# Hybrid recurrent decoder step: columns and decays read in place, TensorE's filler groups moved, the mLSTM mask between two corner updates

## The reference

```python
# mLSTM: qc, kc, vc of a chunk, stabilised decays w, wi, ws
wqk = w * einsum('bthd,bshd->btsh', qc, kc)
num = einsum('btsh,bshd->bthd', wqk, vc) + wi * einsum('bthk,bhkv->bthv', qc, C)
den = sum(wqk) + wi * einsum('bthk,bhk->bth', qc, n)
h = num / max(abs(den), 1)
C = decay * C + einsum('bsh,bshk,bshv->bhkv', ws, kc, vc)
# gated delta rule
lmat = where(strict, einsum('bhtk,bhsk->bhts', kb, kh) * exp(diff), 0)
sol = triangular_solve(eye + lmat, [v * beta, kb * exp(g)])   # unit lower triangular
v_new = u - wk @ S
o = (q * exp(g)) @ S + attn @ v_new
S = S * exp(gl) + (k * exp(gl - g))^T @ v_new
# HGRN2
o = (q * exp(G)) @ S + attn @ v;   S = exp(Gl) * S + (k * exp(Gl - G))^T @ v
```

## Time and profile before

| what | value |
|---|---|
| runs, median (lowest to highest) | 3650.18 us (3647.09 to 3650.99) |
| profiled execution: its own time | 3649.81 us |
| profiled execution: its span | 3648.0 us |
| busy over the span, PE / DVE / ACT / POOL | 90% / 50% / 39% / 12% |
| `prompt_mixers`, tiles 0 to 15 in the trace | about 985 to 1740 us of the span |

### The profile page before, as it was taken

The page is one execution under the profiler, slowest core; times in us unless marked ns, Lnnn a source line. Parts: engine busy times, 40 slices in busy tenths (PEclk is TensorE's granted clock), DMA queues, the critical chain, the costliest instruction groups (busy, mean ns, idle before and its releaser), DMA issues. The chain is left out here.

```text
span 3648.0 us, 52370 instructions
## 1 busy us (share of the span) xinstructions
PE 3287.7 (90%) x21605; PEld 2988.0 (82%) x21605; DVE 1829.2 (50%) x2931; ACT 1416.9 (39%) x2100; POOL 436.4 (12%) x450
## 2 busy tenths in 40 slices
PE   5899999998289999897559979999999999999998
PEld 4899999998278888886538769999999999999987
DVE  6232333221378888885447734454454454454465
ACT  6233422322155555552025533343343343343454
POOL 0000000000156556651300000000000000000000
PEclk6899999999699999998579989999999999999999
DMA  5222233221622223221135564334444354344353
GB/s 194 50 60 67 70 72 83 83 71 57 255 76 93 96 89 98 88 75 44 39 138 214 186 234 163 133 144 153 149 173 153 118 186 150 133 146 154 133 202 116
DMA packets 232386, 450.24 MB, mean 123 GB/s; under 512 B 41383, under 2 KB 115293, under 8 KB 228029
## 3 DMA queue, kind: packets, MB, share of 16 engines
q1 hardware_dynamic: 230020, 428.33, 34.9%
q10 hardware_dynamic: 2128, 18.56, 1.4%
HBM read 363.38 MB, written 83.47 MB: 122 GB/s over the span
## 5 line engine op out<-in xcount | busy, mean ns | idle before, releaser
L2769 PE MATMUL ff_p<-ff_h_hi,ff_w_hi 128*128 128x384 f32 (+1 forms) x1536 | 502.6, 327 | 23.4 <-DMA ff_h_lo<-tmp_h 23.4
L2771 PE MATMUL ff_p<-ff_h_hi,ff_w_lo 128*128 128x384 f32 (+1 forms) x1536 | 502.8, 327 | 0.0
L2770 PE MATMUL ff_p<-ff_h_lo,ff_w_hi 128*128 128x384 f32 (+1 forms) x1536 | 501.9, 327 | 0.0
L412 PE MATMUL pin_pz<-hi,pin_whi 128*128 128x424 f32 (+1 forms) x1320 | 469.4, 356 | 14.2 <-DVE pin_wlo L528 14.2
L413 PE MATMUL pin_pz<-lo,pin_whi 128*128 128x424 f32 (+1 forms) x1320 | 467.2, 354 | 0.0
L414 PE MATMUL pin_pz<-hi,pin_wlo 128*128 128x424 f32 (+1 forms) x1320 | 467.0, 354 | 0.0
L2788 PE MATMUL ff_p<-ff_w_lo,ff_f_hi 128*128 128x512 f32 (+1 forms) x1088 | 426.7, 392 | 0.0
L2789 PE MATMUL ff_p<-ff_w_hi,ff_f_lo 128*128 128x512 f32 (+1 forms) x1088 | 426.4, 392 | 0.0
L2787 PE MATMUL ff_p<-ff_w_hi,ff_f_hi 128*128 128x512 f32 (+1 forms) x1088 | 423.8, 389 | 0.0
L2872 DVE TENSOR_TENSOR ff_w_lo<-ff_w,ff_w_hi 128x1024 fp32r<-128x1024 f32 x192 | 235.2, 1225 | 345.6 <-ACT ff_w_hi L2820 345.6
L2820 ACT ACTIVATE ff_w_hi<-ff_w 128x1024 fp32r<-128x1024 f32 x192 | 203.6, 1060 | 388.9 <-PE ff_p L2789 384.6
(11 more groups left out here) (522 smaller groups left out, 5536.5 us busy)
## 6 DMA issues: line engine op xcount, KB each, us to landing
ff_w<-in_w_unit SPq DMA_DIRECT2D x192, 512.0 KB, 5.2
ff_w<-in_w_unit SPq DMA_DIRECT2D x48, 2048.0 KB, 7.9
tmp_z<-pin_z SPq DMA_DIRECT2D x32, 1024.0 KB, 5.2
mix_rb<-tmp_rows_p SPq DMA_DIRECT2D x16, 1152.0 KB, 5.9
pin_w<-in_w_in SPq DMA_DIRECT2D x33, 512.0 KB, 8.1
gat_wa<-in_w_ada ACTq DMA_DIRECT2D x8, 2048.0 KB, 28.7
mix_zb<-tmp_z SPq DMA_DIRECT2D x16, 640.0 KB, 4.2
tmp_h<-op_h_hi SPq DMA_DIRECT2D x17, 512.0 KB, 4.1
```

The lines of the kernel that those rows point to most:

```text
L412: pe.matmul(pz[:, g, 0:n], whi[:, u, k], hi[:, k, at:at + n], start=(k == 0), stop=False)
L2769: pe.matmul(dst, w1_hi[:, u, k], hi, start=(k == 0), stop=False)
L2770: pe.matmul(dst, w1_hi[:, u, k], lo, start=False, stop=False)
L2771: mm = pe.matmul(dst, w1_lo[:, u, k], hi, start=False, stop=(k == KT - 1))
```

## The change

Four things change, all inside `prompt_mixers`. The arithmetic is the same.

1. `cc` is gone as a tile: it is now a function that gives the slice of `cols_p`, and the readers on VectorE and ScalarE read that slice.
2. `dc` is one tile for all sixteen tiles of tokens, filled once by two copies ahead of the loop. `decays` keeps its wait for `rb` and the addition into `ex`, and nothing else.
3. On TensorE `outputs` and `states` are each split in two, one part ahead of a level's product and one behind it; the transposes of gk and gv are split in the same way around level 4's product; the mLSTM scores move from behind level 5's product to ahead of it.
4. On VectorE the product into `pm` moves from behind `update(5)` to between its x corners and its xt corners.

```diff
-        cc, dc, ex = two("cc", [P, NQ, MH]), [sb(f"dc{k}", [P, 2, 3]) for k in range(3)], two("ex", [P, MH, 2, P])
+        ex, dc = two("ex", [P, MH, 2, P]), sb("dc", [P, 2, TILES, 3])
+        cc = lambda t, q: keep["cols_p"][:, q, t * MH:(t + 1) * MH]
...
-                def outputs():
+                def hgrn_state():
                     pe.wait_ge(S("kd"), b(1, 1))
                     pe.wait_ge(S("vn"), b(1, 1))
-                    for h in range(MH):
-                        pe.matmul(pc[:, 1, h * HD:(h + 1) * HD], at_[:, h, :], vn[:, h, :], start=True, stop=True)
                     for par in range(2):
                         for j in range(2):
                             at = MH * HD + j * HD
-                            mm = pe.matmul(pc[half(par), 1, at:at + HD], kd[:, 2 * j + par, :], hv[:, 2 * j + par, :],
-                                           start=True, stop=True)
+                            pe.matmul(pc[half(par), 1, at:at + HD], kd[:, 2 * j + par, :], hv[:, 2 * j + par, :],
+                                      start=True, stop=True)
+
+                def outputs():
+                    for h in range(MH):
+                        mm = pe.matmul(pc[:, 1, h * HD:(h + 1) * HD], at_[:, h, :], vn[:, h, :], start=True, stop=True)
                     mm.then_inc(S("av"), 1)
...
+                if not first:
+                    hgrn_state()
+                if not tail:
                     level_product(2)
                 if not first:
                     outputs()
                 if not tail:
                     level_update(2)
+                if not first:
+                    delta_state()
+                if not tail:
                     level_product(3)
                 if not first:
-                    states()
+                    mlstm_state()
                 if not tail:
                     level_update(3)
+                    turn(pd, [A[:, A_GK + j, :] for j in range(3)], done=False)
                     level_product(4)
                     pe.wait_ge(zb_in[u], 32 * (r + 1))
-                    turn(pd, [A[:, A_GK + j, :] for j in range(3)] + [B[:, B_GV + j, :] for j in range(3)])
+                    turn(pd, [B[:, B_GV + j, :] for j in range(3)], 3)
                     level_update(4)
-                    level_product(5)
                     if not first:
                         pe.wait_ge(S("cm"), b(1, 2))
                     heads(pc, B[:, B_MK:B_MV], A[:, A_MQ:A_GQ], "qk_m")
+                    level_product(5)
                     pe.wait_ge(S("tok_d"), v(3, 2))
...
+            for par in range(2):
+                dve.tensor_copy(dc[half(par)], dec[half(par), :, :, 3 * par:3 * par + 3])
...
-            def decays(t, u, r, then):
+            def decays(t, u, r):
 
                 dve.wait_ge(rb_in[u], 16 * (r + 1))
-                dve.tensor_scalar(cc[u][:], keep["cols_p"][:, :, t * MH:(t + 1) * MH], 1.0, None, ALU.mult)
-                for par in range(2):
-                    ins = dve.tensor_scalar(dc[t % 3][half(par)], dec[half(par), :, t:t + 1, 3 * par:3 * par + 3]
-                                            .rearrange("p w o j -> p w (o j)"), 1.0, None, ALU.mult)
-                then(ins)
                 dve.tensor_tensor(ex[u][:], rb[u][:, :, 0:2, :], late[:, 0:1, :].unsqueeze(1).broadcast_to([P, MH, 2, P]),
                                   ALU.add).then_inc(S("exa"), 1)
...
-                def update(l):
+                def update(l, between=lambda: None):
...
                         ins.then_inc(S("x"), 1)
+                    between()
                     dve.wait_ge(S("u"), v(U, 2 * l))
...
-                    update(5)
-                    dve.wait_ge(S("qk_m"), v(1, 1))
-                    dve.tensor_tensor(hm(pm[:]), pv(pc, P), hm(ex[u][:, :, 0, :]), ALU.mult).then_inc(S("pm"), 1)
+                    update(5, mlstm_scores)
```

More of the change, by code:

```diff
@@ L1729, in corners @@
             return [(slice(at + n, at + 2 * n), slice(at, at + n)) for at in range(0, P, 2 * n)]
-        colh = lambda u, q, w: cc[u][:, q, :].rearrange("p (r j) -> p r j", r=2).unsqueeze(3).broadcast_to([P, 2, 3, w])
+        colh = lambda t, q, w: cc(t, q).rearrange("p (r j) -> p r j", r=2).unsqueeze(3).broadcast_to([P, 2, 3, w])
         tok = lambda b, at: b.rearrange("p a (j r c) -> p (a j) r c", r=2, c=HD)[:, at:at + 3].rearrange("p j r c -> p r j c")
@@ L1823, in heads, with turn @@
                     mm.then_inc(S(done), 1)
-                def turn(dst, rows):
-                    for n, row in enumerate(rows):
+                def turn(dst, rows, at=0, done=True):
+                    for n, row in enumerate(rows, at):
                         mm = pe.transpose(dst[:, n // 4, (n % 4) * P:(n % 4 + 1) * P], row, keep["ident"][:])
-                    mm.then_inc(S("turned"), 1)
+                    if done:
+                        mm.then_inc(S("turned"), 1)
                 def six(dst, lhs, rhs, done, n=2 * P):
@@ L1887, in outputs, with delta_state @@
                             at = MH * HD + j * HD
-                            mm = pe.matmul(pc[half(par), 1, at:at + HD], kd[:, 2 * j + par, :], hv[:, 2 * j + par, :],
-                                           start=True, stop=True)
+                            pe.matmul(pc[half(par), 1, at:at + HD], kd[:, 2 * j + par, :], hv[:, 2 * j + par, :],
[3 more added lines that the diff above has]
+                        mm = pe.matmul(pc[:, 1, h * HD:(h + 1) * HD], at_[:, h, :], vn[:, h, :], start=True, stop=True)
                     mm.then_inc(S("av"), 1)
-                def states():
+                def delta_state():
                     for h in range(MH):
@@ L1895, in states, with mlstm_state @@
                         pe.matmul(pc[half(par), 0, j * HD:(j + 1) * HD], gkw[:, h, :], vn[:, h, :], start=True, stop=True)
+                def mlstm_state():
                     for h in range(MH):
@@ L2034, in decays @@
                     for k in range(2):
-                        ins = act.activation(ex[u][:, h, k, :], ex[u][:, h, k, :], ACT.Exp, bias=cc[u][:, Q_A + k, h:h + 1])
+                        ins = act.activation(ex[u][:, h, k, :], ex[u][:, h, k, :], ACT.Exp, bias=cc(t, Q_A + k)[:, h:h + 1])
                 if heads[-1] == MH - 1:
@@ L2224, in chain @@
                 return then, count
-            def decays(t, u, r, then):
+            def decays(t, u, r):
                 dve.wait_ge(rb_in[u], 16 * (r + 1))
-                dve.tensor_scalar(cc[u][:], keep["cols_p"][:, :, t * MH:(t + 1) * MH], 1.0, None, ALU.mult)
-                for par in range(2):
-                    ins = dve.tensor_scalar(dc[t % 3][half(par)], dec[half(par), :, t:t + 1, 3 * par:3 * par + 3]
-                                            .rearrange("p w o j -> p w (o j)"), 1.0, None, ALU.mult)
-                then(ins)
                 dve.tensor_tensor(ex[u][:], rb[u][:, :, 0:2, :], late[:, 0:1, :].unsqueeze(1).broadcast_to([P, MH, 2, P]),
                                   ALU.add).then_inc(S("exa"), 1)
-            decays(0, 0, 0, chain("step0", 0)[0])
+            decays(0, 0, 0)
             def body(t, u, r, first=False, last=False, tail=False):
@@ L2279, in update, with mlstm_scores @@
                     ins.then_inc(S("xt"), 1)
+                def mlstm_scores():
+                    dve.wait_ge(S("qk_m"), v(1, 1))
+                    dve.tensor_tensor(hm(pm[:]), pv(pc, P), hm(ex[u][:, :, 0, :]), ALU.mult).then_inc(S("pm"), 1)
                 if not first:
@@ L2290, in body @@
                         ins = dve.scalar_tensor_tensor(rv[:, h, :], pc[:, h // 3, (h % 3) * HD:(h % 3 + 1) * HD],
-                                                       cc[o][:, Q_NBEG, h:h + 1], bv[:, h, :], ALU.mult, ALU.add)
+                                                       cc(t - 1, Q_NBEG)[:, h:h + 1], bv[:, h, :], ALU.mult, ALU.add)
                     ins.then_inc(S("rv"), 1)
-                    dve.tensor_tensor(yg, pv(pc, HD, 3 * HD), colh(o, Q_EG, HD), ALU.mult).then_inc(S("qs_read"), 1)
+                    dve.tensor_tensor(yg, pv(pc, HD, 3 * HD), colh(t - 1, Q_EG, HD), ALU.mult).then_inc(S("qs_read"), 1)
                     dve.wait_ge(S("mo"), b(1, 1))
-                    then(dve.tensor_tensor(hm(num[:]), pv(pd, W, 3 * W), colh(o, Q_WI, W), ALU.mult))
+                    then(dve.tensor_tensor(hm(num[:]), pv(pd, W, 3 * W), colh(t - 1, Q_WI, W), ALU.mult))
                     dve.tensor_tensor(hm(num[:]), hm(num[:]), pv(pd, W), ALU.add).then_inc(S("num"), 1)
@@ L2307, in body @@
                 if not last:
-                    decays(t + 1, 1 - u, r + u, then)
+                    decays(t + 1, 1 - u, r + u)
                 if not tail:
@@ L2331, in body @@
                     dve.wait_ge(S("dg"), b(1, 1))
-                    dl = dc[(t - 1) % 3]
+                    dl = dc[:, :, t - 1, :]
                     for j in range(3):
@@ L2345, in body @@
                     dve.wait_ge(S("turned"), v(2, 1))
```

(10 more changed lines are left out.)

## The result

| | median | runs |
|---|---|---|
| before | 3650.59 us | 3641.07 to 3656.53, six runs |
| changed | 3623.04 us | 3619.56 to 3631.95, six runs |

The ratio is 0.9932, with a 95% interval from 0.9913 to 0.995. The forecast was 3624 us. The profiled execution has a span of 3622.6 us against 3648.0.

A forecast was written before the change was run, and what follows sets the result against it. No engine is full; a chain hopping between engines bounds each turn. Fourteen turns at 1.7 us (1.08 plus 0.62) give 23.8, with the end tiles 26 us together, from 3649.8 to 3624 us; range 3611 to 3637.

The forecast's parts named there:

- The copies come back only as 1.08 us a turn: VectorE's addition into ex, held until GpSimd's hk ends, then 1.62 us: gain 1.08 us, not the copies' 4.3.
- Rival 1: At ex on VectorE: nothing is held by GpSimd, 2.97 us a turn gained, 3606 us; chance 0.10.
- pm is worth 0.62 us a turn: VectorE's pm between the corner updates lets y's transposes start earlier: 0.62 us beyond the 1.08, bounds 0 and 0.78.
- The ends: First and last tiles, lacking part of the gain: tile 0 taken as 1.0 us, the last tile as 1.2 us.
- The filler groups are worth 0: TensorE's groups moved ahead of level products fill 0.28 us waits; delays are covered by VectorE or bv: gain 0.
- About two lost turns at 3.95 us each: Turns where VectorE's y product is held through GpSimd's run: about two again, as before, each costing 3.95 us.
- rival 3: VectorE loses the race at y in twelve more turns, costing 47 us: 3671 us; chance 0.05 of ending above before.

The follow-up runs named there:

- e1: Changed kernel with only columns and decays read in place, TensorE's groups and pm as before the change: 3653.20 us, ratio 1.001 to before.
- e10: Columns and decays read in place only, plus GpSimd's differences for the next tile placed after VectorE's scaling of y: 3628.84 us, ratio 0.9947 to before.
- e5: Changed kernel, with GpSimd's large hk product started only after VectorE's addition into ex: 3624.52 us, ratio 0.9935 to before.
- e6: Changed kernel, with GpSimd's large hk product split into two instructions of 4 and 3 levels: 3610.16 us, ratio 0.9899 to before.
- e4: Changed kernel, with the per-tile cc and dc copies kept on VectorE: 3637.54 us, ratio 0.9967 to before.
- e2: Changed kernel, with the product into pm back behind both corner updates: 3636.88 us, ratio 0.9968 to before.
- e9: Kernel before, with GpSimd's differences for the next tile placed after VectorE's scaling of y: 3643.29 us, ratio 0.9983 to before.
- e12: Changed kernel, with only the mLSTM scores back behind level 5's product on TensorE: 3639.20 us, ratio 0.9963 to before.
- e3: Changed kernel, with all of TensorE's groups back in the order of before: 3634.10 us, ratio 0.9971 to before.
- e11: Changed kernel with TensorE's groups in the old order, plus GpSimd's differences placed after VectorE's scaling of y: 3622.81 us, ratio 0.9933 to before.
- e7: Changed kernel, with GpSimd's differences for the next tile placed after VectorE's scaling of y: 3622.65 us, ratio 0.993 to before.

## Why the prediction was right, and where it was not

1. **The copies come back only as 1.08 us a turn.** Right: 1.07 in e1 and e10. One step of its path needed more than ex: level 3's identity products were to begin 1.08 us earlier, and they do (17.25 us into the turn against 18.34), but only with the groups moved. In e10, where these are in their old places, they begin at 17.57, behind TensorE's own filler groups, and the turn still gains 1.07, so the chain ran through VectorE and not through that wait. That ex would be held to the end of hk and then run 1.62 us is in the trace to the hundredth. Rival 1 (nothing is held) is out; e5 and e6 show the hold by moving and by splitting it. The Trainium skill's rule on the pair that VectorE and GpSimd share (SBUF — State Buffer, "Who interferes with whom"), that a VectorE instruction with two SBUF inputs and one of GpSimd that reads SBUF exclude each other, held for ex in e1, e5, e6 and the changed kernel, with 4.96 us for an instruction that takes 1.75 alone.
2. **pm is worth 0.62 us a turn.** It measured 0.58 (e4) and 0.55 (e2). Right. The two terms together give 1.65 in the ordinary turn, against 1.7.
3. **The ends.** Tile 0 gave 1.15 us (41.69 to 40.54 from the first lt to the second) for the 1.0 taken. The last tile's 1.2 us stays unconfirmed. From the last lt to the last y the time fell from 60.6 to 58.9 us, but that stretch lasts between 56.2 and 61.6 us over all the kernels, and e9, whose order there is that of the kernel before, took 57.1 with the granted clock at 0.93 in place of 0.89.
4. **The filler groups are worth 0.** This is the step that failed, though not in the ordinary turn, where they give 0.05 us. The prediction saw that the scores would set level 5's product back and that bv would cover it for TensorE. It did not follow the same delay through ScalarE's exponentials to GpSimd, where moving it changes how long a held y is held. By the medians e12 puts 11 to 16 us on it and e3 11 us (with all groups back), of which their profiles show 8.4 and 4.9 between first and last lt; in e11, where y is never held, nothing of it is left to see.
5. **About two lost turns at 3.95 us each** (rival 3). The price was read off the kernel before (4.41 and 4.42 us, turns of 47.3) and is partly the clock's: e3's turns show 2.4 us at a clock of 1.00 and 3.5 at 0.96. In the changed kernel there were five, of which four cost 0.6 to 0.7 us and one 3.8: 6.4 us in all instead of 7.9. More were lost, each was cheaper, and so the total came out as forecast. That the number agrees to 1 us is in this part luck: with the scores left in place, the prediction's own sum would have said 3624 for a kernel that measures 3639.

What stays open is why a waiting y loses at all. It asks at the same point to within 0.06 us in nearly all turns, about 0.14 us into one of GpSimd's short products, and wins or loses there. In the profiles the turns that lose have no starting point of their own. No run here tells why six of e1's ten runs are 10 to 31 us longer than its profiled one. They had a lower granted clock over the whole execution, 0.940 to 0.946 against 0.948 to 0.949 in the other four. In e11, where GpSimd's differences wait for y in every run and so cannot hold it, two of six runs took 3634 to 3635 us at 0.945 against 3619 to 3623 at 0.950. So lost turns are not the only thing that can lengthen a run, and how much of a median's difference is theirs is not shown.

## What to carry to other kernels

A tiny copy on VectorE that took microseconds was here a sign of GpSimd, and removing it gave back only what was not held by the next instruction of the same kind; look at GpSimd's instruction beside it and shorten that (e6: one product cut in two, 13 us). An instruction with a median of 1.3 and a maximum of 4.4 us was here a race, and an edit elsewhere changed its price by more than the edit's own worth. To value such edits, first take the race away (e7 to e11), then compare turns of the same granted clock and not only medians.

## What the runs showed of the hardware that was not expected

- A VectorE instruction held behind a run of GpSimd instructions does not surely get in at the next boundary. Mostly it did (y 1.34 us, and ex between the two parts of hk in every turn of e6); at times it was passed over at four boundaries in a row, for 3.2 us, although it had been waiting all along (4.42 us against 1.21 alone).
- Of the y's that were still waiting when bd's turn came, 15 of 17 got in ahead of it where bd had become ready only 0.08 to 0.18 us before, and 0 of 12 where it had been ready for 0.69 to 0.72 us. The two that did not get in had 0.18 us, as had one that did, so at that distance something else decides. That the readiness of GpSimd's next instruction is the cause is argued from these distances and from e12, which moves them; it was not varied by itself.
- What a held instruction costs depends on TensorE's clock in the same turn: a y of 4.4 us cost 2.4 us at a granted clock of 1.00 (e3, two turns) and 3.3 to 4.0 at 0.96 (before, changed, e1, e3, e12). A turn at 0.96 without a held y was up to 1.5 us longer (e5, e10, e11).
